# Two experts' rows spread by TensorE instead of stored and loaded back, in a two-layer hybrid trunk with a hierarchical mixture of experts

## The reference, cut to what matters

```python
def hierarchical_moe(h, wc, bc, wf, bf, w_gate_up, w_down):
...
    e_w = jax.nn.softmax(e_logit, axis=-1) * g_prob
    expert_id = g_idx * EXPERTS_PER_GROUP + e_idx
    gates = jnp.sum(jax.nn.one_hot(expert_id, N_EXPERTS, dtype=jnp.float32) * e_w[..., None], axis=1)
    gu = jnp.einsum('nd,edf->nef', xt, w_gate_up)
    gate, up = jnp.split(gu, 2, axis=-1)
    act = jax.nn.silu(gate) * up * gates.astype(h.dtype)[..., None]
    return jnp.einsum('nef,efd->nd', act, w_down).reshape(b, t, d)
...
        x = x + hierarchical_moe(h, router_c_w[layer], router_c_b[layer], router_f_w[layer], router_f_b[layer],
                                 moe_w_gate_up[layer], moe_w_down[layer])
    return rms_norm(x, final_norm_w)
```

## Time and profile before

| | us |
|---|---|
| median of 3 runs | 1181.36 (1177.66 to 1183.61) |
| the profiled execution | 1181.09 |
| its span, first to last instruction | 1179.3 |

### The profile page before, as it was taken

How to read it: one execution, slowest core, us unless ns; L and a number is a source line. 1 busy time by engine, 2 the same in 40 slices (tenths; PEclk the granted TensorE clock), 3 DMA queues, 4 the chain that set the end, 5 groups by cost and what they waited for, 6 DMA issues and landing times.

```text
span 1179.3 us, 19724 instructions
## 1 busy us (share of the span) xinstructions
PE 1111.8 (94%) x7062; PEld 912.1 (77%) x7063; DVE 701.5 (59%) x1016; ACT 608.6 (52%) x903; POOL 405.1 (34%) x344
## 2 busy tenths in 40 slices
PE   8999999999998899998999999999999997999980
PEld 5778887778787688886788888888888886888870
DVE  5435444367736999996646341543442138999975
ACT  5556234242434699995633342233342234899871
POOL 4343121110133244442155325442244442344442
PEclk8999999999999899999999999999999997999995
DMA  9333311112225699996443213331222364999955
GB/s 262 79 86 56 72 38 55 37 44 66 72 68 210 244 353 375 379 364 238 174 128 98 81 56 106 97 106 56 81 73 91 104 190 161 354 388 374 358 208 223
DMA packets 89859, 194.76 MB, mean 165 GB/s; under 512 B 20348, under 2 KB 21432, under 8 KB 89016
## 3 DMA queue, kind: packets, MB, share of 16 engines
q1 hardware_dynamic: 67560, 159.34, 40.6%
q10 hardware_dynamic: 12432, 17.60, 4.4%
q0 software_dynamic: 9792, 16.80, 3.8%
HBM read 189.50 MB, written 23.07 MB: 180 GB/s over the span
## 4 chain that ended last, share of the span: by engine, by line
PE 80%; DVE 8%; DMA 5%; ACT 3%; issue 2%; ACTq 1%; SPq 0%; POOL 0%; POOLq 0%; DVEq 0%
PE ps L674 23%; PE ps L676 22%; PE ps L675 22%; PE ps L2570 2%; PE ps L2362 2%; DMA raw<-in_moe_w_down_dram 1%; DMA arena<-y 1%; DVE x L1467 1%; PE ps L2245 1%; ACTq L1421 1%; PE ps L2498 1%; DMA arena<-hs,slot_rows 1%; PE ps L2199 1%; ACT wh L1007 1%; DMA y<-arena,cur_rows 1%
## 5 line engine op out<-in xcount | busy, mean ns | idle before, releaser
L841 POOL TENSOR_TENSOR wl<-raw,wh 128x1024 fp32r<-128x1024 f32 x94 | 228.6, 2440 | 380.5 <-ACT wh L1007 380.2
L674 PE MATMUL ps<-wh,hT_hi 128*128 128x512 f32 x864 | 346.7, 401 | 3.5 <-DVE hT_lo L1986 2.4
L676 PE MATMUL ps<-wh,hT_lo 128*128 128x512 f32 x864 | 337.9, 391 | 0.0
L675 PE MATMUL ps<-wl,hT_hi 128*128 128x512 f32 x864 | 337.2, 390 | 0.0
L1007 ACT ACTIVATE wh<-raw 128x1024 fp32r<-128x1024 f32 x116 | 122.4, 1068 | 212.6 <-PE ps L676 191.0
L674 PEld LDWEIGHTS ps<-wh,hT_hi 128*128 128x128 f32 x864 | 162.8, 188 | 39.1 <-issue 3.5
L676 PEld LDWEIGHTS ps<-wh,hT_lo 128*128 128x128 f32 x864 | 162.3, 188 | 34.6
L675 PEld LDWEIGHTS ps<-wl,hT_hi 128*128 128x128 f32 x864 | 162.8, 188 | 30.9
L674 PE MATMUL ps<-hT_hi,wh 128*128 128x512 f32 (+1 forms) x296 | 116.9, 395 | 2.1 <-DVE arena_rounded L1818 1.0
L1961 DVE TENSOR_TENSOR wl<-arena,wh 128x1024 fp32r<-128x1024 f32 x96 | 113.8, 1222 | 4.7 <-ACT wh L1294 3.1
L1961 DVE TENSOR_TENSOR wl<-raw,wh 128x1024 fp32r<-128x1024 f32 x92 | 109.5, 1223 | 8.2 <-ACT wh L1294 5.4
(11 more groups left out here) (331 smaller groups left out, 1576.8 us busy)
## 6 DMA issues: line engine op xcount, KB each, us to landing
raw<-in_moe_w_gate_up_dram SPq DMA_DIRECT2D x64, 512.0 KB, 11.5
arena<-in_moe_w_gate_up_dram SPq DMA_DIRECT2D x64, 512.0 KB, 10.5
raw<-in_odd_w_in_dram SPq DMA_DIRECT2D x48, 512.0 KB, 3.7
raw<-in_even_w_in_dram SPq DMA_DIRECT2D x32, 512.0 KB, 4.8
arena<-in_moe_w_down_dram SPq DMA_DIRECT2D x32, 512.0 KB, 11.7
raw<-in_moe_w_down_dram SPq DMA_DIRECT2D x32, 512.0 KB, 14.1
raw<-in_odd_w_out_dram SPq DMA_DIRECT2D x16, 512.0 KB, 3.6
arena<-y ACTq DMA_DIRECT2D x6, 1024.0 KB, 9.9
```

What stands on the lines that cost most here:

```text
L674: nc.tensor.matmul(dst, lh, rh, start=first, stop=False)
L675: nc.tensor.matmul(dst, lh, rl, start=False, stop=False)
L676: return nc.tensor.matmul(dst, ll, rh, start=False, stop=last)
L841: pool.tensor_tensor(columns_of(i, wl[:, i % NSPL, :, :]), raw_columns(i), columns_of(i, wh[:, i % NSPL, :, :]).bitcast(F32), ALU.subtract ...
```

## The change

The last two experts of a layer (14 and 15, `LAST = NE - 2`) are not scattered to `y2_dram` any more. Their rows stay in SBUF, weighted by `w_slot`, the weight of the token in each slot: ACT stores the weights of all pairs to a small DRAM tensor after the second expert, and POOL gathers two columns of them after the fourth. ACT's copy out of PSUM writes the high half `late_hi`, DVE makes the low half (`late_low`). `slot_tokens` on DVE makes, for each of the two experts, a 128 x 512 mask that is one where a slot belongs to a token. `late_rows(l, T)` on PE multiplies mask and rows, 8 matmuls for each tile of tokens, into two PSUM banks, and `add_late` on DVE adds them to `X`. The other 14 experts' rows are loaded by SP as soon as expert 13's scatter has landed. Their weights `w_early` are zero where a pair went to a late expert; so that such rows of `y2_dram`, which nothing writes, hold finite numbers, the tensor, now one for both layers, is cleared once by a DMA of 4 MB during block 1 of layer 0.

Moved with it: the low halves of block 10's first four pieces go from DVE to POOL; the high halves of the first two of them go ahead of ACT's last two copies out of PSUM; the `keep_busy` matmuls of `norm(2)` are gone, and so is SP's wait for the loaded rows ahead of later weight pieces.

```diff
-    return i in DVE_LO or any(m + 2 <= i < m + 6 * NE for m in MOE_PIECE) or first_piece(10) <= i < first_piece(10) + 4
+    return i in DVE_LO or any(m + 2 <= i < m + 6 * NE for m in MOE_PIECE)
...
-        y2_dram = [nc.dram_tensor(f"y2{l}", (2 * SEQ, DM), F32, kind="Internal").ap() for l in range(2)]
+        w_dram = [nc.dram_tensor(f"w{l}", (2 * SEQ, 1), F32, kind="Internal").ap() for l in range(2)]
+        y2_dram = [nc.dram_tensor("y2", (2 * SEQ, DM), F32, kind="Internal").ap()] * 2
...
-        YP = reg(12288, 8192).rearrange("p (b j d) -> p b j d", b=4, j=2)
+        LAST = NE - 2
+        YP = [reg(at, 2048).rearrange("p (j d) -> p j d", j=2) for at in (0, 2048, 4096, 14336)]
+        no_rows = reg(21760, 512)
+        late_hi, late_lo = v3(rounded(9216, 2048), 2), v3(rounded(7168, 2048), 2)
+        over_x, over_y = over_xt[:, :], over_yt[:, :]
+        slot_token = [tokens[:, 512 * e:512 * e + 512] for e in range(2)]
...
+        w_early, w_slot, token_at = small[:, 420:428], small[:, 428:430], v3(small[:, 430:438], 2)
...
+            def load_early_rows(l):
+
+                for q in range(2):
+                    sp.wait_ge(s_(f"y_stored{q}"), 112 * (l + 1))
+                src = y2_dram[l].rearrange("(T p j) d -> T p j d", p=P, j=2)
+                sp.dma_start(YP[0][:, 0, :], src[0][:, 0, :]).then_inc(s_("yp_loaded0"), 16)
+                sp.dma_start(YP[0][:, 1, :], src[0][:, 1, :]).then_inc(s_("yp_second0"), 16)
+                for T in range(1, NT):
+                    sp.dma_start(YP[T], src[T]).then_inc(s_(f"yp_loaded{T}"), 16)
...
+            load_early_rows(0)
             overflow_sp(sp, 0)
-            sp.wait_ge(s_("yp_loaded3"), 16)
...
+                def late_experts():
+
+                    pool.wait_ge(s_("w_stored"), 16 * (l + 1))
+                    for e in range(2):
+                        rows = idx[:, 1, LAST + e:LAST + e + 1].bitcast(U32)
+                        pool.indirect_dma_start(out=w_slot[:, e:e + 1], out_offset=None, in_=w_dram[l],
+                                                in_offset=bass.IndirectOffsetOnAxis(ap=rows, axis=0),
+                                                bounds_check=last_pair_row, oob_is_err=False).then_inc(s_("late_ready"), 16)
...
                 two_experts(0)
-                with pool.Fori(1, NE // 2 - 1) as it:
+                two_experts(1)
+                late_experts()
+                with pool.Fori(2, NE // 2 - 2) as it:
                     two_experts(it)
                 for par in range(2):
...
-                    pool.wait_ge(s_(f"xg_loaded{q}"), 144 * (l + 1))
+                    pool.wait_ge(s_(f"y_stored{q}"), 112 * (l + 1))
+                    pool.nop().then_inc(s_("ysb_free"), 1)
...
+                    if last and par == 1:
+                        hi(m + 6 * NE)
+                        hi(m + 6 * NE + 1)
                     act.wait_ge(s_("ysb_free"), E + 1)
+                    if last:
+                        act.wait_ge(s_("late_ready"), 32 * (l + 1))
                     for hf in range(2):
+                        c = slice(512 * hf, 512 * hf + 512)
                         act.wait_ge(used, it * 12 + (6 * NE * l + 6 * par + 4 + n0 + hf + 1))
-                        act.activation(ysb[:, par, 512 * hf:512 * hf + 512], ps[:, 2 + hf, :], ACT.Copy).then_inc(s_("y_read"), 1)
-                        if hf == 0 and not last:
+                        if last:
+                            act.activation(late_hi[:, par, c], ps[:, 2 + hf, :], ACT.Copy, scale=w_slot[:, par:par + 1]).then_inc(s_("y_read"), 1)
+                            continue
+                        act.activation(ysb[:, par, c], ps[:, 2 + hf, :], ACT.Copy).then_inc(s_("y_read"), 1)
...
+                    if n == 1:
+                        act.wait_ge(s_("w_ready"), l + 1)
+                        with nc.allow_non_contiguous_dma(reason="two weights of a token"):
+                            act.dma_start(w_dram[l].rearrange("(T p j) o -> p T (j o)", p=P, j=2), v3(w12, 4)).then_inc(s_("w_stored"), 16)
...
-                for i in range(4):
+                for i in range(2, 4):
                     hi(m + 6 * NE + i)
...
+                    if step[1] == 4:
+                        act.wait_ge(s_("y_cleared"), 16)
...
+                    if step[1] == 1:
+                        act.wait_ge(s_("no_rows_set"), 1)
+                        act.dma_start(y2_dram[0].rearrange("(p n) (k c) -> p (n k) c", p=P, c=512), no_rows.unsqueeze(1).broadcast_to([P, 16, 512]))\
+                            .then_inc(s_("y_cleared"), 16)
...
+                D(dve.memset(no_rows, 0.0), s_("no_rows_set"))
...
-                D(stt(X[:, T, :], YP[:, T, j, :], w12[:, 2 * T + j:2 * T + j + 1], X[:, T, :], ALU.mult, ALU.add),
-                  s_(f"moe_added{l}") if j == 1 else None)
+                D(stt(X[:, T, :], YP[T][:, j, :], w_early[:, 2 * T + j:2 * T + j + 1], X[:, T, :], ALU.mult, ALU.add))
...
+            def late_low(l, e, hf):
+
+                c = slice(512 * hf, 512 * hf + 512)
+                dve.wait_ge(s_("late_ready"), 32 * (l + 1))
+                dve.wait_ge(s_("y_read"), 32 * l + 31 + 2 * e + hf)
+                stt(late_lo[:, e, c], ps[:, 2 + hf, :], w_slot[:, e:e + 1], late_hi[:, e, c].bitcast(F32), ALU.mult, ALU.subtract)\
+                    .then_inc(s_("late_low_made"), 1)
+
+            def add_late(l, T):
+
+                dve.wait_ge(s_("late_rows"), 4 * l + T + 1)
+                b = late_banks(l, T)
+                D(tt(v3(X[:, T, :], 2), v3(X[:, T, :], 2), ps[:, b:b + 2, :], ALU.add), s_(f"moe_added{l}"))
...
+                if n in (2, 4):
+                    l = n // 2 - 1
+                    combine(l, 0, 0)
+                    late_low(l, 1, 0)
+                    late_low(l, 1, 1)
+                    combine(l, 0, 1)
+                    add_late(l, 0)
+                    combine(l, 1, 0)
+                    combine(l, 1, 1)
+                    add_late(l, 1)
                 if n == 2:
-                    for i in range(4):
-                        lo(first_piece(10) + i)
-                    combine(0, 0, 0)
-                    combine(0, 0, 1)
-                    combine(0, 1, 0)
-                    combine(0, 1, 1)
                     dve.wait_ge(s_("wb_loaded"), 32)
-                    for T in range(NT):
+                    lo_tiles(("hT", n, 0), 0)
+                    for T in range(1, NT):
+                        if T + 1 < NT:
+                            combine(0, T + 1, 0)
+                            combine(0, T + 1, 1)
+                            add_late(0, T + 1)
                         lo_tiles(("hT", n, T), T)
...
-                    for T in range(NT):
+                    dve.wait_ge(s_("wb_loaded"), 64)
+                    for T in (2, 3):
                         for j in range(2):
                             combine(1, T, j)
-                        if T == 2:
-                            dve.wait_ge(s_("wb_loaded"), 64)
-                            last(0)
-                    last(1)
+                        add_late(1, T)
+                        last(T - 2)
...
+            def slot_tokens():
+
+                D(ts(slots_u, slotA, 1, None, ALU.logical_shift_right))
+                D(ts(w_early, slots_u, LAST // 2, None, ALU.not_equal))
+                D(tt(w_early, w_early, w12, ALU.mult))
+                D(tt(token_at, idx[:, 0, LAST:NE].unsqueeze(2).broadcast_to([P, 2, NT]),
+                     offs16[:, 0:NT].unsqueeze(1).broadcast_to([P, 2, NT]), ALU.subtract))
+                for e in range(2):
+                    D(tt(v3(slot_token[e], NT), iotaB.unsqueeze(1).broadcast_to([P, NT, P]),
+                         token_at[:, e, :].unsqueeze(2).broadcast_to([P, NT, P]), ALU.is_equal), s_("slot_token_made"))

             def xT_lo(l, e, par):
...
+                    if last:
+                        late_low(l, 0, par)
+                    if last and par == 1:
+                        slot_tokens()
...
+            def late_rows(l, T):
+
+                if T == 0:
+                    pe.wait_ge(s_("slot_token_made"), 2 * (l + 1))
+                elif T > 1:
+                    pe.wait_ge(s_(f"moe_added{l}"), T - l)
+                b = late_banks(l, T)
+                for e in range(2):
+                    pe.wait_ge(s_("late_low_made"), 4 * l + 2 * e + 2)
+                    for hf in range(2):
+                        c = slice(512 * hf, 512 * hf + 512)
+                        mm(ps[:, b + hf, :], slot_token[e][:, cols(T)], late_hi[:, e, c], start=e == 0, stop=False)
+                        ins = mm(ps[:, b + hf, :], slot_token[e][:, cols(T)], late_lo[:, e, c], start=False, stop=e == 1)
+                ins.then_inc(s_("late_rows"), 1)
...
                 if n == 2:
-                    keep_busy(22)
+                    late_rows(0, 0)
+                    late_rows(0, 1)
                 for T in range(NT):
```

(11 more changed lines are left out.)

106 lines of the change are left out of this document (57 added, 49 removed).

## The result

The changed kernel takes 1188.29 us (median of 11 runs, 1184.93 to 1192.49), the kernel before in the same runs 1181.11. The ratio is 1.0068, with an interval from 1.0053 to 1.0084: slower by 0.7%, or 8 us. The forecast was 3.4 us more.

A forecast was written before the change was run, and what follows sets the result against it. The prediction took the chains of work at two boundaries, between the layers and at layer 1's end, to bound the kernel. +5.2 and -1.8 sum to +3.4 on the profiled 1181.09, giving 1184.5 us, range 1175.0 to 1189.0.

The forecast's parts named there:

- The sign: Whole kernel: the change was forecast to make it slower, by 3.4 us.
- rival B: Block 10's first rows begin at PE's low clock, 3 us more, +6.4 in all, 1187.5; chance 0.20.
- At nothing: Items priced at no cost, among them the 4 MB clear, ACT's small store and POOL's gathers in the experts.
- The block by POOL: Between the layers, POOL's four splits hold DVE's `slot_tokens`, one instruction per split; second mask 8.6 us later.
- The stretch between the layers: From layer 0's last expert to the last tile's transposes: these end 5.2 us later.
- The end of layer 1: Layer 1's last combines and squares, with no POOL splits: 1.8 us sooner.
- So no combine waits for rows: Between the layers, rows loaded after expert 13's scatter land by about 546 to 549, in time for DVE's combines.
- rival A: Between the layers, POOL's splits hold DVE not at all or only briefly: -4.1 there, -5.9 in all, 1175.3; chance 0.30.

The follow-up runs named there:

- the four runs above: Layer 0's experts, one execution each: changed kernel 159.6 us; without store and gathers 157.6; with 13 instead of 10 idle matmuls 158.1; without the store, gathers kept, 156.0.
- rows_first: Changed kernel with POOL's splits behind the masks, store in 128 packets, and two tiles' rows loaded ahead of block 10's third and fourth pieces: 1182.94 us.
- warm: Changed kernel with POOL's splits behind the masks and 20 unread matmuls on PE between the two experts' parts of the first `late_rows`: 1185.80 us.
- warm_short: Changed kernel with POOL's splits behind the masks and 11 unread matmuls on PE between the two experts' parts of the first `late_rows`: 1183.30 us.
- best: Changed kernel with POOL's splits behind the masks, store in 128 packets, and 13 instead of 10 idle matmuls ahead of each layer's first expert: 1179.28 us.
- masks_early: Changed kernel with `slot_tokens` moved into the experts, behind `pair_weights`, and the store in 128 packets: 1184.07 us.
- both: Changed kernel with POOL's splits behind the masks and the store in 128 packets: 1181.20 us.

## Why the prediction was wrong

The sign was right, and the time lies inside the range of 1175 to 1189, but the change is 8 us where 3.4 was forecast. Slower by over 0.5% had been given a chance of 0.27. That the time lies near rival B's 1187.5 is chance: in the changed kernel B's cost is absent, and a cost that no rival had stands in its place.

- **The step that failed** is "At nothing: ... ACT's small store and POOL's two small gathers, since both engines wait for PE in the experts". I priced the engines that issue, which did have the time, and not the DMA engines that carry it out, which had little. The store cost 3 to 4.5 us over both layers: 4.5 back without store and gathers, 3.2 without the store, 3.9 more for a second one, and 3.7 by the experts of the profiles. That the DMA engines are 95% busy through layer 0's experts was in the profile of the kernel before.
- **Missing altogether** is the clock at the start of the experts: 1.5 us in layer 0 by the four runs above. No instruction there was changed. That three more idle matmuls ahead of them bring it back is shown; why the changed kernel loses it is not. Store and clock together are some 5 of the experts' 6.6 us. The rest stays open: without the store the experts still take 2.4 more than in the kernel before, of which the clock in layer 0 is a part, and in layer 1, where it is no part, 158.0 and 158.3 stand beside 157.0. The unrolled pair on POOL and the shared `y2_dram` were not tried apart.
- **The block by POOL** was right in place and size. The second mask was to end 8.6 later than undisturbed; with POOL's splits behind the masks it ends 3.2 after the last activations' low half began, in the changed kernel 11.6 after, 8.4 more. Four instructions each waited out one split, as forecast. The rows said it. The Trainium skill, page "SBUF — State Buffer", section "Who interferes with whom", says it too: a VectorE operation with two SBUF inputs contends with GpSimd for the port they share, and one whose other input is in PSUM doesn't. The trace agrees, with 2.27 beside 0.17, and 1.22 for an add inside a split. L2030, a tensor_scalar with one input in SBUF, waited as well.
- **The stretch between the layers** was to be 5.2 longer and is 4.6. The first rows matmul was to come at 569.3; it came at 572.74, which less the 3.9 us by which the last low half came later (546.75 for 542.81) is 568.8.
- **The end of layer 1** was to be 1.8 shorter, of which 0.7 were charged ahead of the mark used here, so 2.5 by this mark; it is 2.9 shorter. `add_late` took 1.22 (forecast 1.27), `late_low` 0.75 (0.78). The four items of DVE's new work there add up to 10.35, not the 10.5 that I wrote, which nothing else used.
- **"So no combine waits for rows"** was wrong, and hidden by the block: with the splits behind the masks, or the masks early, one waited 1.3 to 3.4 us, for pieces of weights that lay ahead of the rows (rows_first). It would have cost rival A a part of its gain.
- **Rival A** (1175.3) is out in this kernel, and even with the masks free the stretch takes 34.6 at best, not the 30.7 that A's 4.1 would give, since the first combine then waits for rows and the combines pay for the splits.
- **Rival B** is out in both profiles of the changed kernel: the rows begin at 0.23 to 0.24 us a matmul. PE's late matmuls did run at the low clock (0.43), beside DVE's chain. Its mechanism is real, though: in six variants (warm, warm_short, best, masks_early, both and rows_first) the clock falls just ahead of the first rows or in them, and costs 1.2 to 2.2 us.

## What to carry to other kernels

A transfer is priced by what the DMA engines do at that moment, not by its bytes or by the idle time of the engine that issues it: where the DMA engines are 95% busy with the weights' stream, two stores of 4 KB in 512 packets, one in each layer, cost some 3 to 4 us together. A place ahead of the stream gave 3.2 of them back by the medians; a quarter of the packets gave 2.8, of which the experts' stages show 0.9. Work given from VectorE to GpSimd isn't free for VectorE while it has instructions with two inputs in SBUF: the block goes to whichever stand there next, so count them all, and put those with a PSUM input beside the splits. When a stretch is made shorter, look at TensorE's granted clock again: it was unharmed in the changed kernel and fell in most of the variants that were meant to mend it. And what is hidden by one wait must be priced as if that wait were gone, since taking it away brings it out.
